# Half of a weight remainder by an accumulating transfer in six slots a chunk, and three seven-product steps in every chunk from the third

## What is computed

```
def swiglu(h, wg, wu, wd):
    return (jax.nn.silu(h @ wg) * (h @ wu)) @ wd
x = x + 0.5 * swiglu(rmsnorm(x, ffn1_norm[i]), ffn1_wg[i], ffn1_wu[i], ffn1_wd[i])
x = x + hybrid_mixer(...)
x = x + 0.5 * swiglu(rmsnorm(x, ffn2_norm[i]), ffn2_wg[i], ffn2_wu[i], ffn2_wd[i])
```

## Time and profile before

| | |
|---|---|
| median of three runs | 1814.15 us |
| span of the profiled execution, first to last instruction | 1810.6 us |
| TensorE, VectorE, ScalarE, POOL busy | 99%, 86%, 56%, 14% |
| memory read over the span | 350.11 MB |

### The profile page before, as it was taken

How to read it: one execution, slowest core, us unless ns; L and a number is a source line. 1 busy time by engine, 2 the same in 40 slices (tenths; PEclk the granted TensorE clock), 3 DMA queues, 4 the chain that set the end, 5 groups by cost and what they waited for, 6 DMA issues and landing times.

```text
span 1810.6 us, 21958 instructions
## 1 busy us (share of the span) xinstructions
PE 1799.3 (99%) x8134; PEld 1481.8 (82%) x8134; DVE 1555.0 (86%) x1863; ACT 1022.7 (56%) x1334; POOL 246.2 (14%) x442
## 2 busy tenths in 40 slices
PE   9999999999999999999999999999999999999998
PEld 7788888888888888888788888888888888888886
DVE  7999998889999977678667867899999889999987
ACT  6655555445555556556567745555555455555554
POOL 1111111001111100000123300111111000222100
PEclk9999999999999999999999999999999999999999
DMA  7676766667676766766443655667676666677764
GB/s 244 209 213 221 217 210 211 207 202 220 206 216 203 218 201 207 209 214 194 149 138 107 209 174 185 209 207 218 209 216 212 214 207 194 209 219 221 242 202 151
DMA packets 199289, 367.28 MB, mean 203 GB/s; under 512 B 19013, under 2 KB 23857, under 8 KB 199057
## 3 DMA queue, kind: packets, MB, share of 16 engines
q1 hardware_dynamic: 185008, 352.37, 62.5%
q0 software_dynamic: 11648, 12.02, 2.2%
q10 hardware_dynamic: 2528, 1.52, 0.3%
HBM read 350.11 MB, written 4.19 MB: 196 GB/s over the span
## 4 chain that ended last, share of the span: by engine, by line
PE 93%; DVE 5%; ACT 1%; DMA 1%; issue 0%; ACTq 0%; DVEq 0%
PE ps L771 23%; PE ps L773 23%; PE ps L772 23%; PE ps L789 7%; PE ps L791 7%; PE ps L790 7%; PE ps L838 2%; DVE w_lo L1820 2%; DVE wt_lo L1892 1%; DVE wt L1882 0%; ACT w_hi L1305 0%; PE ps L1069 0%; PE ps L1096 0%; DMA raw<-in_ffn_wu_dram 0%; PE ps L1071 0%
## 5 line engine op out<-in xcount | busy, mean ns | idle before, releaser
L1820 DVE TENSOR_TENSOR w_lo<-raw,w_hi 128x1024 fp32r<-128x1024 f32 x573 | 692.1, 1225 | 111.8 <-ACT w_hi L1305 107.8
L1305 ACT ACTIVATE w_hi<-raw 128x1024 fp32r<-128x1024 f32 x573 | 599.6, 1056 | 287.3 <-PE ps L773 197.8
L771 PE MATMUL ps<-w_hi,hT_hi 128*128 128x512 f32 x1308 | 512.4, 392 | 1.3 <-ACT gu L1399 1.2
L773 PE MATMUL ps<-w_hi,hT_lo 128*128 128x512 f32 x1308 | 509.6, 390 | 0.0
L772 PE MATMUL ps<-w_lo,hT_hi 128*128 128x512 f32 x1308 | 509.3, 389 | 0.0
L712 POOL DMA_DIRECT2D gu_raw<-gu_sq x352 | 187.5, 541 | 1077.2 <-DVE gu_sq L2066 1003.7
L1356 ACT ACTIVATE wt_hi<-wt 128x1024 fp32r<-128x1024 f32 x164 | 172.9, 1054 | 274.7 <-DVE wt L1882 274.7
L771 PEld LDWEIGHTS ps<-w_hi,hT_hi 128*128 128x128 f32 x1308 | 245.7, 188 | 52.0 <-ACT gu L1399 2.1
L773 PEld LDWEIGHTS ps<-w_hi,hT_lo 128*128 128x128 f32 x1308 | 245.6, 188 | 52.0
L772 PEld LDWEIGHTS ps<-w_lo,hT_hi 128*128 128x128 f32 x1308 | 245.7, 188 | 49.7
L1892 DVE TENSOR_TENSOR wt_lo<-wt,wt_hi 128x1024 fp32r<-128x1024 f32 x164 | 199.6, 1217 | 0.0
(11 more groups left out here) (312 smaller groups left out, 2219.6 us busy)
## 6 DMA issues: line engine op xcount, KB each, us to landing
raw<-in_ffn_wu_dram SPq DMA_DIRECT2D x176, 512.0 KB, 4.5
raw<-in_ffn_wd_dram SPq DMA_DIRECT2D x176, 512.0 KB, 4.8
raw<-in_ffn_wg_dram SPq DMA_DIRECT2D x175, 512.0 KB, 4.1
raw<-in_w_in_dram SPq DMA_DIRECT2D x88, 512.0 KB, 3.6
raw<-in_w_out_dram SPq DMA_DIRECT2D x32, 512.0 KB, 4.2
gu_raw<-gu_sq POOLq DMA_DIRECT2D x352, 32.0 KB, 3.5
x_parked<-x SPq DMA_DIRECT2D x8, 256.0 KB, 5.3
raw<-in_cmp_k_w_dram SPq DMA_DIRECT2D x8, 256.0 KB, 3.2
```

The lines of the kernel that those rows point to most:

```text
L771: mm(o, x_hi, w_hi[:, s, kk, :], start=begin, stop=False, skip_group_check=skip)
L773: ins = mm(o, x_lo, w_hi[:, s, kk, :], start=False, stop=last and kk == GK - 1, skip_group_check=skip)
L1305: act.activation(w_hi[:, c % SLOTS, :, :], raw[:, c % SLOTS, :, :], ACT.Copy).then_inc(hi_ready, 1)
L1820: tt(w_lo[:, s, :, :], raw[:, s, :, :], w_hi[:, s, :, :].bitcast(F32), ALU.subtract).then_inc(lo_ready, 1)
```

## The change

It does two things.

**Three pairs in all chunks from the third.** `THREE` becomes 2 to 10, so chunks 3, 7 and 9 take the order of `CHUNK3` in place of `CHUNK`, and they belong to `LATE`.

**Half of the remainder by a transfer.** In every chunk in `THREE`, in the slots 0, 1, 10, 11, 14 and 15 (`MOVED_AT`), the remainder of the half `kk` = 1 isn't made by VectorE. ScalarE first writes the negated weight, rounded to fp32r, into `w_lo`, and then `w_hi` as before. POOL waits for that and issues a transfer of 256 KB that reads the weight from memory once more and adds it to what stands in `w_lo`. VectorE subtracts on the half `kk` = 0 alone. TensorE waits for the transfer between the two halves of the slot. There are 9 x 6 x 2 = 108 such slots. POOL's loop is written out, so that the transfers of slots 0 and 1 are issued before the 16 of the chunk before, and those of slots 10 to 15 after them.

```diff
-THREE = (2, 4, 5, 6, 8, 10)
+THREE = (2, 3, 4, 5, 6, 7, 8, 9, 10)
+MOVED_AT = (0, 1, 10, 11, 14, 15)
...
+def moved_slots():
+
+    return [FFN0[f] + chunk_slot(n) + p for f in range(2) for n in THREE for p in MOVED_AT]
+
+
+def moves(c):
+
+    return sum(1 for m in MOVED if m <= c and m % SLOTS == c % SLOTS)
...
+        minus_ready = sem("minus_ready")
+        lo_moved = [sem(f"lo_moved{s}") for s in range(SLOTS)]
...
+            def remainder(f, n, p):
+
+                c = FFN0[f] + chunk_slot(n) + p
+                s, (kind, q) = c % SLOTS, chunk_table(n)[p]
+                w = (wg if kind == GATE else wu)[f]
+                pool.wait_ge(minus_ready, MOVED.index(c) + 1)
+                pool.dma_start(w_lo[:, s, 1, :], w[:, GK * q + 1, n * CH:n * CH + CH],
+                               accum_op=ALU.add).then_inc(lo_moved[s], 16)
+
             def ffn(f):
-                with pool.Fori(0, NFC - 1) as i:
-                    gu_blocks(f, 0, i)
-                gu_blocks(f, NFC - 1)
+                for n in range(1, NFC):
+                    early = [p for p in MOVED_AT if p < 3] if n in THREE else []
+                    late = [p for p in MOVED_AT if p >= 3] if n in THREE else []
+                    for p in early:
+                        remainder(f, n, p)
+                    if n != PART0[1]:
+                        gu_blocks(f, n - 1)
+                    for p in late:
+                        remainder(f, n, p)
+                    if n == PART0[1] - 1 or n == NFC - 1:
+                        gu_blocks(f, n)
...
                 for kk in range(GK):
+                    if kk and c in MOVED:
+                        pe.wait_ge(lo_moved[s], 16 * moves(c))
...
+                if c in MOVED:
+                    act.activation(w_lo[:, c % SLOTS, 1, :], raw[:, c % SLOTS, 1, :], ACT.Copy,
+                                   scale=-1.0).then_inc(minus_ready, 1)
...
-                tt(w_lo[:, s, :, :], raw[:, s, :, :], w_hi[:, s, :, :].bitcast(F32),
+                own = 1 if c in MOVED else GK
+                tt(w_lo[:, s, 0:own, :], raw[:, s, 0:own, :], w_hi[:, s, 0:own, :].bitcast(F32),
                    ALU.subtract).then_inc(lo_ready, 1)
```

More of the change, by code:

```diff
@@ L195 @@
 END = FFN0[1] + FFN_GROUPS
+MOVED = moved_slots()
 OUT0 = AT[("out", 1), 0]
```

## The result

The changed kernel took 1853.41 us (median of four runs, 1847.35 to 1859.47) beside 1814.26 us for the kernel before (1813.94 to 1816.62): a ratio of 1.0215, interval 1.0203 to 1.0227. It is 39 us slower. The forecast was 1810.0 with a range up to 1823. What came is rival C: the landing is the last wait at slot 10.

A forecast was written before the change was run, and what follows sets the result against it. TensorE was taken as the bound, with VectorE close behind. New pairs -4.1 us, stalls at most -0.6 and late landings +0.6 summed to -4.1 us, a forecast of 1810.0 us, range 1809.0 to 1823.0.

The forecast's parts named there:

- rival C: At slot 10 the landing becomes the last wait once it passes about 5.5 us; 1822.7 to 1841 us; chance 0.26.
- Part 1: Three pairs in chunks 3, 7 and 9 of both FFNs: TensorE loses 3 matmuls in each, saving 4.1 us.
- Part 3: ScalarE's 108 negations at 615 ns, 66 us in all, fit its free time; second SiLU moves 0.22 us, within cover.
- rival D: Slot 1's negation makes the second SiLU late, up to 0.6 us in each of 18 chunks: 1821 us; chance 0.03.
- A met wait inside a group: Waiting for an already landed half between a slot's matmuls costs nothing; if wrong at 0.1 us each, 11 us.
- Rival E: The three new steps don't shorten their chunks, as when VectorE is still the last wait: 1814 us; chance 0.03.
- Part 2: VectorE's w_lo halved in 108 slots: 3.25 us relief a chunk, 58.5 us in all; itself saves up to 0.6 us.
- Part 4: POOL's accumulating transfer lands in about 5 us against about 5.5 us of budget at slot 10, just hidden in most slots.
- C's upper case: Landing at 7 us: 18 stalls of 1.5 us at slot 10 plus 18 of 0.2 at slot 14, giving 1841 us.

The follow-up runs named there:

- the kernel without transfers: Changed kernel with the 108 transfers removed, negations and waits kept, so TensorE multiplies the negated weight in those halves; 1810.1 us, ratio 0.9979 to the kernel before.
- slots 0 and 3: Changed kernel with transfers only in slots 0 and 3 of each three-pair chunk, 36 in all; 1809.8 us, ratio 0.9977 to the kernel before.
- no relief: Changed kernel with three pairs in all chunks from the third but no transfers, every remainder on VectorE; 1819.8 us, ratio 1.0030 to the kernel before.
- plain transfer: Changed kernel with a plain load of the same bytes in place of each accumulating transfer; 1824.8 us, ratio 1.0063 to the kernel before.
- not awaited: Changed kernel with transfers running but TensorE not waiting, multiplying the high part twice there; 1829.5 us, ratio 1.0081 to the kernel before.
- slot 10 alone: Changed kernel with one transfer a chunk, at slot 10, 18 in all; 1844.4 us, ratio 1.0176 to the kernel before.

## Why the prediction was wrong

**Where it was right.** TensorE as the bound and VectorE as the engine behind it held. Part 1's -4.1 us is what the kernel without transfers shows (-4.0) and what slots 0 and 3 keep (-4.3). Part 3 held: the negation takes 621 ns where 615 were taken, and the second SiLU leaves 1.1 us of cover behind chunk 4 where 0.9 were asked for, so rival D did not appear. A met wait inside a group costs nothing, as assumed. Rival E fell with the same runs.

**Part 2 was right in kind and generous in size.** VectorE's chunk fell from 41.3 us (no relief) to 38.4 (no transfer), 2.9 where 3.25 were forecast. What I didn't ask is how much of it was needed. About 1 us is enough, and the other 2 were bought at dear places.

**Part 4 failed, by two terms of its sum.** First, the landing, "I take about 5 us with a spread, which is just hidden in most slots": measured 6.1 in slot 10 and 6.5 over all six. The row taken for the move, 4.6 us of the earlier trace rows, was not too low: the plain transfer lands after 4.2 in slot 10. What was mis-sized is the addition, "for which I add up to 1 us", of which the 5 kept half: it takes 1.9. Second, "So I take 5 to 6 us of budget, about 5.5 in most chunks": measured 3.2 to 5.5, median 4.6, in the 16 chunks that paused. The same count over the old kernel's ten such slots gives 4.0 to 6.0, median 5.4, so 5.5 was right for the old kernel; the new one, even without transfers, has a median of 4.8. That three pairs in every chunk leave each one less of a lead is the likely reason and isn't shown by itself. For it: in the old kernel chunk 5, the only one right behind a chunk with three pairs, had 4.5 and 4.7. Against it: the 4.0 of the earlier trace rows stood behind a chunk with two. On top comes POOL's 0.3 us from the negation to the issue, which the prediction did not have.

The margin was forecast as 5.5 - 5 = +0.5 us. It came out as 4.6 - 0.3 - 6.1 = -1.8 us by the medians, and as 4.3 - 0.3 - 5.8 = -1.8 in the chunk shown. Two errors of about 1 us each against half a microsecond of margin.

**Two more steps were too light.** The prediction priced slot 10, with 0.2 us for slot 14 in C's upper case, and let the others pass as less tight; by the table above slots 11 and 14 have only 0.4 and 0.5 us more. And "SP's loads will land somewhat later. In most slots that is covered": those of slots 2 to 4 land 2 to 3 us later, 3 to 4 where TensorE doesn't wait for the transfers, and there it isn't covered. At slot 9, where it was feared, the load lands after 5.1 us in place of 4.9.

**Rival C, priced right and weighted low.** It said 18 x 0.7 at 6.2 us and 18 x 1.5 at 7 us, 1822.7 to 1841. With the measured landing and the budget of 5.5 it gives 1828. The rest is what it did not have: the shorter budget, 15 us of pauses outside slot 10 (it had 3.6 for slot 14 in its upper case), and about 7 us of lower clock, which lie partly in these. The sentence "the tightest of the six is slot 10" was true, but slot 11 has only some 5.4 us itself once slot 10 doesn't stall. And the range ended at 1823, with C's upper case, 1841, worked out and then left out of it.

The Trainium skill ("DMA: Bandwidth & Descriptors", anatomy of one DMA on the GpSimd path) has 2.0 us plus bytes over 436 GB/s, 2.6 us for this transfer as an estimate. The plain transfer took 5.3 here beside a load stream of over 200 GB/s (3.1 at the least), and a quarter of it, with the addition, 4.6. This case's traces don't agree with the fit, and the measurement decides.

**What stays open.** How far the landing of 6.5 us is queueing behind SP's 512 KB loads wasn't tried apart: no kernel ran the transfers with fewer of those loads. That the transfers delay the loads is read from the traces: with plain transfers the loads of slots 2 to 4 are late too (7.0, 7.6 and 7.7 us), with slots 0 and 3 less so (5.1, 6.2 and 6.9), and with slot 10 alone they are not (4.6, 4.8 and 5.0). What the delay alone would cost at each number of transfers wasn't tried. Nor was a slower clock's share in the four runs' scatter measured by more than their mean clocks.

## What to carry to other kernels

A transfer that replaces engine work is hidden or not by one subtraction at the tightest place, landing less budget, and both terms have to be read under the load and in the neighbourhood that the changed kernel will have, not the old one's. Move first only as much as the bound engine needs, and put it where the slack is widest: here 2 halves a chunk in slots with 8 us gave -0.23%, while a single one in a slot with 4.5 us gave +1.8%. A wait taken out of one place tells nothing until the next places are looked at, since its pause was their slack: here it hid three more tight slots and the late loads of the weight stream. So read the budgets in a kernel in which nothing pauses.

## What the runs showed of the hardware

- An accumulating transfer of 256 KB issued by POOL landed 6.5 us after its issue (4.1 to 8.7), the same one without the addition after 5.3; a quarter of it, with the addition, after 4.6. In one and the same slot, slot 10, it was 6.1, 4.2 and 4.3 us.
- Its issue took 847 ns of POOL against 531 for the plain one, and its bytes 1.8 times the DMA engines' time.
- With six such transfers a chunk, SP's 512 KB loads of slots 2 to 4 landed 6.8 to 8.3 us after their issue (as changed) and 7.9 to 9.5 (not awaited), where they took 4.9 to 5.5 without transfers.
- From the end of the negation to POOL's next issue passed 0.30 us, in nearly all slots.
- Behind some pauses of TensorE amid dense work came a granted clock of 0.50, with matmuls 0.43 us apart in place of 0.227, and about 1.7 us more were lost. Of the pauses in the chunks of these kernels none up to 1.94 us was followed by it, three of the six from 1.96 to 2.01 us were, and five of the six longer ones. The longest, 3.55 us, was the exception.
